# A mixture-of-experts layer: three of five token tiles take their experts from a streamed table instead of gathered rows

## The chip, the cores and the metric

The kernel runs on one core of one Trainium2 chip. The metric is the device time of one execution in microseconds, the median of several. The engines are TensorE (PE; PEld is its weight load), VectorE (DVE), ScalarE (ACT), GpSimd (POOL) and SyncE (SP), which issues DMAs.

## The reference, cut to what matters

One layer of a hybrid backbone for 128 context tokens (tile 0) and 512 latent tokens (tiles 1 to 4), D = 1024, everything in fp32: a gated linear recurrence and an attention, mixed and projected, then PEER, an expert layer with 16384 experts. Only PEER is touched:

```python
def per_block(xb):                                        # 128 tokens
    q = (xb @ w_q).reshape(n, P_HEADS, 2, P_QDIM // 2)    # 8 heads, two halves
    s = jnp.einsum('nhpd,hpkd->nhpk', q, sub_keys)        # 128 keys a half
    s1, i1 = lax.top_k(s[:, :, 0], 16); s2, i2 = lax.top_k(s[:, :, 1], 16)
    ...                                                   # best 16 of the 16 x 16 sums
    idx = jnp.take_along_axis(cand_i, pos, axis=-1)       # expert = i1 * 128 + i2
    g = jax.nn.softmax(top_s, axis=-1)
    u = jnp.take(w_u, idx, axis=0)
    act = jax.nn.gelu(jnp.einsum('nhkd,nd->nhk', u, xb), approximate=False)
    v = jnp.take(w_v, idx, axis=0)
    return jnp.einsum('nhk,nhkd->nd', (g * act), v)
```

Each token so takes 8 x 16 = 128 experts, and the result is the sum over them of gate times gelu(u . x) times v. Around it stand x + gate2 * PEER(...) and a final RMSNorm.

## The kernel before, in words

A slot is one rank of one head for the 128 tokens of a tile: 128 slots a tile, 640 in all. For a slot GpSimd gathers one row of `uv` (u and v side by side, 8 KB) for each token with an indirect DMA (L1213, L1235), 1 MB. VectorE makes the dot of u with the token (L1412), ScalarE its gelu and the product with the gate (L957, L963). The v part is added either by VectorE (L1440) or by TensorE: ScalarE puts the weights on a diagonal (L973), and two products of 128x512 with the gathered rows add up in PSUM (L587, L600).

Before a slot stands the routing of its head on VectorE, in 12 parts (L1347 to L1390): the best 16 of each half, their sums, the best 16 of those, the experts' numbers and the softmax, whose exponential ScalarE makes (L952). It needs the scores, which TensorE makes in `post`.

The program runs through these stages, each engine with its own copy of the order:
- modulation rows, tile 0's projections, mixers, output products and expert scores (`post(0)`);
- projections and mixers of tiles 1 to 4, with the 128 slots of tile 0 beside them. `plan_groups` writes the list of TensorE's groups and a place in it for each slot (`SLOT_AT`, from the shares in `STAGES`), and `Beside` calls the slots at these places on every engine;
- `post(1)` for tile 1 and `post(2)` for tiles 2 to 4: output products (`y`, L859), the normed tile turned (`x2T`, L869), queries (`qp`, L877) and scores (`ss`, L888), with the first 64 slots of tile 1 beside them;
- loops over the other 448 slots (L808 to L833, and their like on PE, ACT and POOL), 32 slots a pass, with eight gather buffers, and for each tile the end: gate, sum with x, RMSNorm, store (`tile_end`, L1685).

Weights come in slabs of 1 MB through a ring of three (`RING`), in the order of `SLABS`. SyncE issues a slab when the last group that reads the ring's place is done (L544).

Of the kernel before, what the change touches and what calls it, by code (L numbers as in the profile page):

```python
# [35 lines left out]
P = 128  # L36
# [18 lines left out]
NGA, NGC, NGB = 4, 6, 8  # L55
HSTATIC = 4
NPE = HSTATIC * TOPK // 2
HSLOTS = 2 * TOPK
# [11 lines left out]
BATCHES = [(0,), (1,), (2, 3, 4)]  # L70
MIXES = [(0,), (1, 2, 3, 4)]
NSLOT = TSLOT + HSTATIC * TOPK
# [6 lines left out]
FIRST_ODD = 9  # L79
# [9 lines left out]
POOL_LEAD, PE_LAG = 3, 2  # L89
# [3 lines left out]
for _b in range(len(BATCHES)):  # L93
    if _b < len(MIXES):
        for _q in range(4):
            SLABS += [("gate_a", _b, _q), ("gate_b", _b, _q), ("wo", _b, _q)]
    SLABS += [("wout", _b, _q) for _q in range(4)] + [("wpq", _b, _q) for _q in range(8)]
    if _b == 0:
        SLABS += [("winTL", w, m) for w in WIN_T for m in range(2)] + [("winL", w, a) for w, a in WIN]

# [19 lines left out]
def turn_order(tiles):  # L120

    order = []
    for i in range(len(tiles) + 1):
        order.extend([("x2T", tiles[i])] if i < len(tiles) else [])
        order.extend([("h2", tiles[i - 1])] if i else [])
    return order


def plan_groups():
# [73 lines left out]
    for b in (1, 2):  # L203
        marks.append(len(names))
        post(b)
    marks.append(len(names))
    marks.insert(-2, names.index(("ss", 1, FIRST_ODD)))
    place, used, fulls, n, six = {}, [0] * 6, [0] * 6, 0, 0
    for name in names:
        kind = name[0]  # L210
        wide = kind in ("xT", "kT", "dS", "qkT", "x2T", "h2") or (kind in ("sc", "pT") and name[1] >= HB)
        if kind in ("oA", "oB"):
            banks = (4 if kind == "oA" else 5,)
        elif six_banks(name):
            banks = (six % 6,)
            six += 1
        else:
# [21 lines left out]
    for (_, count, share), lo, hi in zip(STAGES, marks, marks[1:]):  # L239
        reach = np.cumsum([share[names[i][0]] for i in range(lo, hi)])  # L240
# [14 lines left out]
def build(nc, x_prompt, x_sample, cols, rows, normf_rows, brow, consts, masks, sel, cond_rows, ada_slabs, col_slabs, in_slabs, o_slabs,  # L255
          out_slabs, pq_slabs, uv, state, ckT, cv, y_prompt, y_sample, new_state, new_k, new_v):
    with ExitStack() as ctx:
# [17 lines left out]
        R1 = sb("R1", [P, 4 * D])  # L275
# [5 lines left out]
        RG = sb("RG", [P, 3 * 2 * D])  # L281
        BP = sb("BP", [P, NT * 256 + 6 * 512])
        AB = sb("AB", [P, 12288])
        HG = sb("HG", [P, 5632])
# [4 lines left out]
        CT = sb("CT", [P, P + 640 + NCAND])  # L289
# [6 lines left out]
        hst = sb("hst", [P, 16])  # L296
        ast = sb("ast", [P, 168])
        ZB = sb("ZB", [P, P], BF16)
# [6 lines left out]
        ident, mbias, iota = CT[:, 0:P], CT[:, P:P + 640], CT[:, P + 640:P + 640 + NCAND]  # L305
# [61 lines left out]
        SQ2 = [view(HG, 4096, D), view(HG, D, D), view(HG, D, D)]  # L367
        QP = [view(HG, 5120, 2, P), view(HG, 4096, 2, P), view(HG, 4096, 2, NB[2])]
        X1 = [XP] + [AB[:, 6144 + i * D:6144 + (i + 1) * D] for i in range(4)]
        H2 = [PB[:, 0:D]] + [AB[:, at:at + D] for at in (0, 3072, 4096, 5120)]  # L370
        SC = [R1[:, 0:2048], HG[:, 2048:4096], R1[:, 0:2048], AB[:, 10240:12288], AB[:, 1024:3072]]

        def h_of(b, k):

            return hTp[:, k, :] if b == 0 else hTl[:, k, (BATCHES[b][0] - 1) * P:BATCHES[b][-1] * P]

# [54 lines left out]
        kv_out, state_out, y_out, nf_in, zb_ready = (sem("kv_out"), sem("state_out"), sem("y_out"), sem("nf_in"),  # L431
                                                     sem("zb_ready"))
# [81 lines left out]

        slab_turn, counts = {}, [0] * NSLAB
# [8 lines left out]
        def _(sp):  # L524
            def last_use(key):
# [11 lines left out]

            sp.dma_start(CO[:], cols).then_inc(small_in, 16)
# [1378 lines left out]
```

## Time and profile before

| what | value |
|---|---|
| median of 3 runs | 2538.35 us (2537.91 to 2542.24) |
| profiled execution | span 2543.3 us; the page gives no other time of it |
| TensorE busy | 2005.6 us, 79% |
| TensorE weight load | 1104.9 us, 43% |
| VectorE busy | 1749.4 us, 69% |
| ScalarE busy | 945.2 us, 37% |
| GpSimd busy | 941.2 us, 37% |
| read from HBM | 800.79 MB |
| packets of the gathers' queue | 66.5% of 16 engines' span |
| mean granted clock | 0.924 |

The shares are means over stages with different limits, so the rows below take stretches. A busy TensorE is not TensorE at its peak, since its instructions overlap; the distance between the starts of like groups that follow without a gap is the true cost, and it is read from the rows in order of time. An fp32 product stands in the trace as two records. A record's mean in a group of lines is longer than that distance.

### The profile page before, as it was taken

The numbers are of one execution on the slowest core, as the hardware profiler recorded it, in microseconds if no ns is written. First come the engines' busy times: TensorE is split into PE (matmuls) and PEld (weight loads), VectorE is DVE, ScalarE is ACT, GpSimd is POOL, SyncE is SP. The second block draws the span as 40 slices with busy tenths as digits, with TensorE's granted clock in tenths as the row PEclk, the third lists the DMA queues.
The fourth block names the chain that finished last, engine by engine and source line by source line (L and its number), as shares of the span: only waits on it lengthen the run. The fifth ranks groups of instructions, "written<-read, shape, count | busy, mean of one in ns | idle before, by whom it ended". The sixth has DMA issues, their size and how long they took to land. (4 is left out here: it accounts for less than half of the span.)

```text
span 2543.3 us, 27323 instructions
## 1 busy us (share of the span) xinstructions
PE 2005.6 (79%) x6925; PEld 1104.9 (43%) x6925; DVE 1749.4 (69%) x3969; ACT 945.2 (37%) x2456; POOL 941.2 (37%) x774
## 2 busy tenths in 40 slices
PE   6978898946677798668698776877768787687876
PEld 2577846745566543267455222322223222232222
DVE  2732278886776678767787777777777777777764
ACT  1402145223343434312333444444444444344443
POOL 0020012232222222303233554656545665456654
PEclk9998999977888899879899998999999999999999
DMA  8744678851111389859798999999999999999997
GB/s 317 289 152 154 231 291 322 332 192 67 67 67 60 150 332 337 337 203 401 272 372 317 422 421 393 420 422 422 421 404 415 422 422 421 407 401 421 422 422 330
DMA packets 113299, 805.53 MB, mean 317 GB/s; under 512 B 12596, under 2 KB 14006, under 8 KB 17046
## 3 DMA queue, kind: packets, MB, share of 16 engines
q0 software_dynamic: 93760, 680.96, 66.5%
q1 hardware_dynamic: 17704, 118.17, 12.6%
q10 hardware_dynamic: 1712, 4.98, 0.5%
q8 instruction: 50, 0.82, 0.1%
q14 instruction: 73, 0.60, 0.1%
HBM read 800.79 MB, written 3.28 MB: 316 GB/s over the span
## 5 line engine op out<-in xcount | busy, mean ns | idle before, releaser
L1213 POOL DMA_INDIRECT RG<-in_uv,idxs x264 | 356.5, 1351 | 562.0 <-DVE pl L1440 322.1
L957 ACT ACTIVATE agel<-apre 128x1 f32<-128x1 f32 x640 | 129.3, 202 | 984.6 <-DVE apre L1412 981.2
L600 PE MATMUL pl<-RG,BP 128*128 128x512 f32 x576 | 294.9, 638 | 106.8 <-ACT BP L973 102.3
L600 PE MATMUL pl<-RING,BP 128*128 128x512 f32 x576 | 281.7, 621 | 62.1 <-ACT BP L973 59.6
L1412 DVE CUSTOM_DVE_ANT_0 R<-RG,AB 128x1024 f32<-128x1024 f32 x201 | 246.8, 1230 | 100.8 <-DMA RG<-in_uv,idxs 79.8
L1213 POOL DMA_INDIRECT RING<-in_uv,idxs x168 | 248.9, 1482 | 158.7 <-PE pl L600 69.4
L1412 DVE CUSTOM_DVE_ANT_0 R<-RING,AB 128x1024 f32<-128x1024 f32 x168 | 205.9, 1226 | 95.6 <-DMA RING<-in_uv,idxs 77.2
L625 PE MATMUL pa<-HL,RING 128*128 128x512 f32 (+2 forms) x800 | 243.7, 461 | 4.2 <-DVEq L457 2.6
L600 PEld LDWEIGHTS pl<-RG,BP 128*128 128x128 f32 x576 | 100.1, 192 | 294.5 <-ACT BP L973 214.0
L973 ACT ACTIVATE BP<-CT,wexp 128x128 f32<-128x128 f32 x480 | 192.7, 401 | 51.1 <-PE pl L600 12.9
L600 PEld LDWEIGHTS pl<-RING,BP 128*128 128x128 f32 x576 | 104.3, 194 | 234.2 <-ACT BP L973 139.7
L963 ACT ACTIVATE wexp<-agel,gws 128x1 f32<-128x1 f32 x640 | 188.7, 295 | 22.4 <-ACT agel L957 0.3
L625 PEld LDWEIGHTS pa<-HL,RING 128*128 128x128 f32 x800 | 134.5, 195 | 106.0 <-issue 74.3
L1213 POOL DMA_INDIRECT EB<-in_uv,idxs x88 | 118.3, 1345 | 147.0 <-DVE pl L1440 96.8
L1440 DVE SCALAR_TENSOR_TENSOR pl<-RG,wexp,pl 128x1024 f32<-128x1024 f32 x118 | 151.6, 1285 | 9.6 <-ACT wexp L963 9.5
L1412 DVE CUSTOM_DVE_ANT_0 R<-RG,BP 128x1024 f32<-128x1024 f32 x96 | 117.7, 1226 | 43.4 <-DMA RG<-in_uv,idxs 27.6
L1412 DVE CUSTOM_DVE_ANT_0 R<-EB,AB 128x1024 f32<-128x1024 f32 x67 | 82.4, 1229 | 60.1 <-DMA EB<-in_uv,idxs 58.0
L625 PE MATMUL pa<-RING,AB 128*128 128x256 f32 (+2 forms) x432 | 103.9, 390 | 14.8 <-DVEq L457 10.3
L600 PE MATMUL pl<-HL,BP 128*128 128x512 f32 x192 | 94.9, 617 | 24.9 <-ACT BP L973 22.2
L957 ACT ACT_TABLE_LOAD x86 | 110.3, 1283 | 9.9 <-ACT RING L1096 2.8
L600 PE MATMUL pl<-EB,BP 128*128 128x512 f32 x192 | 98.8, 639 | 11.1 <-ACT BP L973 11.1
L625 PEld LDWEIGHTS pa<-RING,AB 128*128 128x128 f32 (+1 forms) x432 | 82.9, 201 | 34.1 <-issue 17.3
(288 smaller groups left out, 3261.0 us busy)
## 6 DMA issues: line engine op xcount, KB each, us to landing
RING<-in_in_slabs SPq DMA_DIRECT2D x42, 1024.0 KB, 6.0
RING<-in_pq_slabs SPq DMA_DIRECT2D x24, 1152.0 KB, 5.5
RING<-in_ada_slabs SPq DMA_DIRECT2D x16, 1024.0 KB, 5.0
RING<-in_out_slabs SPq DMA_DIRECT2D x12, 1024.0 KB, 9.1
RG<-in_col_slabs POOLq DMA_DIRECT2D x8, 1024.0 KB, 6.9
RING<-in_o_slabs SPq DMA_DIRECT2D x8, 1024.0 KB
RG<-in_uv,idxs POOLq DMA_INDIRECT x297
RING<-in_uv,idxs POOLq DMA_INDIRECT x168
```

Of the source, the lines that this page charges most:

```text
L600: last = nc.tensor.matmul(acc[:, c * 512:(c + 1) * 512], DG[:, k % 2, :], bufs[k % len(bufs)][:, D + c * 512:D + (c + 1) * 512], start=Fal ...
L625: return nc.tensor.matmul(out, l, r, start=s, stop=e)
L957: A(agel[:, par, k:k + 1], apre[:, par, k:k + 1], ACT.Gelu).then_inc(gel_done, 1)
L963: A(wexp[:, par, k:k + 1], agel[:, par, k:k + 1], ACT.Copy, scale=gws[:, par, k:k + 1]).then_inc(w_done, 1)
L973: A(DG[:, i % 2, :], ident, ACT.Copy, scale=wexp[:, par, k:k + 1]).then_inc(dg_done, 1)
L1213: nc.gpsimd.indirect_dma_start(out=bufs[b], out_offset=None, in_=uv, in_offset=bass.IndirectOffsetOnAxis(ap=idxs[:, par, k:k + 1], axis=0) ...
L1412: V.tensor_tensor_reduce(out=SCR[k % 2], in0=buf[:, 0:D], in1=hc, scale=1.0, scalar=0.0, op0=ALU.mult, op1=ALU.add, accum_out=apre[:, par, ...
L1440: V.scalar_tensor_tensor(PL[:, :], (GC[i % NGC] if t else GA[n % NGA])[:, D:2 * D], wexp[:, n // TOPK % 2, n % TOPK:n % TOPK + 1], PL[:, : ...
```

## The change

Tile 0 is computed as before, and tile 1 too, except that all its v sums are made by VectorE, in SBUF, with three gather buffers. Tiles 2 to 4 (`DENSE`, 384 tokens) gather nothing. Expert number i1 * 128 + i2 belongs to chunk c = i2, so there are 128 chunks of 128 experts.
- `U` group of a chunk: eight products of 128x384 give u . x for all 128 experts and 384 tokens; ScalarE's gelu puts it into `AR`, a ring of 42 chunks.
- Gate matrix: for each token TensorE multiplies two one-hot matrices over its 128 chosen experts, 128x128 each, the first one-hot in i1 (GpSimd, `slot_hots`), the second in i2 and weighed by the gate (ScalarE for tiles 2 and 3: Square of the distance, then Relu; VectorE for tile 4). Each product (`G` group, four tokens) is evicted by ScalarE and written to a DRAM buffer, `gates`.
- VectorE multiplies the gelus of 16 chunks with the gates, read back in pieces of 1 MB (`weigh`).
- `V` group of a chunk: six products of 128x512 add up the result of three tiles over all 128 chunks in six PSUM banks.

The three `post` stages become two; tiles 1 to 4 go together. Scores are copied out by ScalarE. x1 of the three tiles goes to DRAM and back. The slots of tile 1 lie beside the V groups, one a chunk.

```diff
-BATCHES = [(0,), (1,), (2, 3, 4)]
+BATCHES = [(0,), (1, 2, 3, 4)]
...
-          ("post1", 0, {"y": 3.5, "x2T": 2.0, "h2": 2.0, "qp": 2.0, "ss": 1.0}),
-          ("queries1", 4, {"qp": 2.0, "ss": 0.1}),
-          ("post2", 60, {"y": 3.4, "x2T": 2.5, "h2": 2.5, "qp": 5.2, "ss": 1.2}))
+          ("post", 0, {}),
+          ("dense", 128, {"V": 1.0, "U": 0.0}))
...
+SLABS += [("dU", p) for p in range(NRING // 2)]
+for _p in range(NCH // 2):
+    SLABS += [("dV", _p)] + ([("dU", _p + NRING // 2)] if _p + NRING // 2 < NCH // 2 else [])
...
+            def gate_slab(b, i):
+                n = b * ND + i
+                if n == 0:
+                    wait_full(sp, ("G", ND - 1, P // 4 - 1))
...
+                if n >= 2:
+                    sp.wait_ge(p_done, n - 1)
+                sp.dma_start(GS[n % 2], gates[b, i]).then_inc(gate_in[n % 2], 16)
...
+            def experts_u(c):
+                w = slab("dU", c // 2)[:, c % 2 * D:(c % 2 + 1) * D]
+                ps = start(("U", c))
+                for k in range(KD):
+                    last = mm(ps[:, 0:DTOK], w[:, k * P:(k + 1) * P], hTl[:, k, P:LAT], k == 0, k == KD - 1)
+                finish(("U", c), last)
+
+            def experts_v(c):
...
+                for i in range(ND):
+                    for x in range(2):
+                        last = nc.tensor.matmul(VACC[i][:, x * 512:(x + 1) * 512], AR[:, c % NRING, i * P:(i + 1) * P],
+                                                w[:, x * 512:(x + 1) * 512], start=c == 0, stop=c == NCH - 1,
+                                                skip_group_check=True)
...
+            def gate_group(i, g):
...
+                for x in range(4):
+                    at = g % 2 * 4 + x
+                    last = mm(ps[:, x * P:(x + 1) * P], OH1[q % 2][:, at, :], OH2[q % 2][:, at, :])
...
             mix(1)
...
             post(1)
-            post(2)
-            beside.rest()
...
+            for c in range(12):
+                experts_u(c)
+            for i in range(ND):
+                turn_slots(i)
+                for g in range(0, P // 4, 4):
+                    for x in range(4):
+                        gate_group(i, g + x)
+                    if i < ND - 1:
+                        experts_u(12 + i * 8 + g // 4)
+            for c in range(NEARLY, NRING):
+                experts_u(c)
...
+            for c in range(0, NCH, 2):
+                experts_v(c)
+                experts_v(c + 1)
+                for n in (c + NRING, c + NRING + 1):
+                    if n < NCH:
+                        experts_u(n)
...
+            def gate_hots(i, q):
...
+                for x in range(ONEHOT):
+                    at = q * ONEHOT + x
+                    step.post(A(to[:, x, :], iota_p, ACT.Square, bias=by[:, 1, at:at + 1]))
+                step.settle()
+                for x in range(ONEHOT):
+                    at = q * ONEHOT + x
+                    step.post(A(to[:, x, :], to[:, x, :], ACT.Relu, bias=by[:, 2, at:at + 1], scale=by[:, 3, at:at + 1]))
+                step.settle(oh2a_ready)
...
+                gate_hots(i, 0)
+                for h in range(PH):
+                    for q in (2 * h, 2 * h + 1):
+                        if q + 1 < P // ONEHOT:
+                            gate_hots(i, q + 1)
+                        gates_out(i, 2 * q)
+                        gates_out(i, 2 * q + 1)
+                    gelu_u(12 + i * PH + h)
+                    expos(turn_of(DENSE[i + 1], h))
...
+            def weigh(b, i):
+                n = b * ND + i
+                dve.wait_ge(act_ready, GBLK * (b + 1))
+                dve.wait_ge(gate_in[n % 2], 16 * (n // 2 + 1))
...
+                    step(V.tensor_tensor(to, to, gate[:, lo:lo + m, :], ALU.mult))
...
+            for i, t in enumerate(DENSE):
+                for h in range(PH):
+                    dve.wait_ge(sc_ready, 2 * PH + 2 * h + 2)
...
+                    route(t, h, 0, 12)
+                slots_of(i)
+            for q in range(P // ONEHOT):
+                gate_hots(ND - 1, q)
```

TensorE's order after the scores of `post(2)`, in the kernel before: the last slots beside the queries (L587) and the first of the loops (L600). `HL` holds the turned tiles, `BP` the diagonal, `RG`, `EB`, `RING` and `HL` the gathered rows, `po` and `pl` the sums in PSUM.

```order
L625 MATMUL pa<-HL,RING 128x384 x8
L587 MATMUL po<-RG,BP 128x512 x2
L625 MATMUL pa<-RING,HG 128x128 x6
L587 MATMUL po<-EB,BP 128x512 x2
L600 MATMUL po<-RING,BP 128x512 x6
L600 MATMUL po<-HL,BP 128x512 x2
```

TensorE's order in the changed kernel, one pair of chunks in the middle of the dense pass and the start of the next: `AB` is the ring of weighed gelus, L972 the V groups, L689 the U groups.

```order
L972 MATMUL po<-RING,AB 128x512 x2
L972 MATMUL pl<-RING,AB 128x512 x2
L972 MATMUL pa<-RING,AB 128x512 x2
L972 MATMUL po<-RING,AB 128x512 x2
L972 MATMUL pl<-RING,AB 128x512 x2
L972 MATMUL pa<-RING,AB 128x512 x2
L689 MATMUL pa<-HL,RING 128x384 x16
L972 MATMUL po<-RING,AB 128x512 x2
```

Two products a slot have become six and eight products a chunk, with nothing of another kind between them.

ScalarE's order in the last slots of the kernel before: gelu, gate, diagonal.

```order
L957 ACTIVATE agel<-apre 128x1
L963 ACTIVATE wexp<-agel,gws 128x1
L973 ACTIVATE BP<-CT,wexp 128x128
L957 ACTIVATE agel<-apre 128x1
L963 ACTIVATE wexp<-agel,gws 128x1
```

ScalarE's order in the changed kernel, one block of 16 tokens of tile 2: `XS` is a buffer of one-hots, `G` the turned slot lists, L1299 the evictions of the gate products, L1259 the gelu of a U group, L1049 the exponential of a head of tile 3.

```order
L1285 ACTIVATE XS<-CT,G 128x128 x8
L1289 ACTIVATE XS<-XS,G 128x128 x8
L1299 ACTIVATE AB<-pa 128x8x64 x2
L1285 ACTIVATE XS<-CT,G 128x128 x8
L1289 ACTIVATE XS<-XS,G 128x128 x8
L1299 ACTIVATE AB<-pa 128x8x64 x2
L1302 DMA gates<-AB 128x8x256
L1259 ACT_TABLE_LOAD
L1259 ACTIVATE AB<-pa 128x384
L1049 ACT_TABLE_LOAD
L1049 ACTIVATE BP<-BP 128x16
```

The one-hots, the evictions, a gelu and the exponential on which VectorE's routing waits stand in one queue.

## Rows read from the trace of the kernel before

**Rows 1.** Busy time by stage (instructions), clock, DMA share, GB/s
```profile
1094.60:1260.00 165.40, 129.84 (x657) 105.82 (x656) 117.47 (x277) 44.49 (x115) 31.25 (x30) 0.87 0.75 290
1260.00:1387.00 127.00, 126.73 (x430) 74.04 (x428) 107.03 (x246) 41.94 (x125) 37.65 (x35) 1.00 0.91 351
1387.00:2531.80 1144.80, 892.49 (x1841) 324.33 (x1841) 818.61 (x1982) 495.78 (x1469) 654.28 (x448) 0.97 1.00 413
```

**Rows 2.** TensorE in order of time: start, length, line, shape, records [idle before]
```profile
1093.78 1.01 PE L894 MATMUL po<-ZB 128*128 128x128 bf16 x8 [27.41 <-DVEq L457]
1094.58 16.55 PE L625 MATMUL pa<-RING,AB 128*128 128x256 f32 x64
...
2502.00 1.98 PE L600 MATMUL pl<-HL,BP 128*128 128x512 f32 x4 [0.50 <-ACT BP L973]
```

**Rows 3.** TensorE in order of time, gapless groups
```profile
229.24 7.31 PE L625 MATMUL pa<-EB,RING 128*128 128x128 f32 x64
...
236.39 3.74 PE L625 MATMUL pa<-HG,RING 128*128 128x128 f32 x32
...
917.96 27.63 PE L625 MATMUL pa<-HL,RING 128*128 128x512 f32 x64
...
945.43 7.03 PE L625 MATMUL po<-AB,RING 128*128 128x512 f32 x16
...
1260.44 5.32 PE L625 MATMUL pa<-HL,RING 128*128 128x384 f32 x16
1265.60 1.88 PE L587 MATMUL po<-RG,BP 128*128 128x512 f32 x4
```

**Rows 4.** TensorE and VectorE in order of time, tile 1's turning
```profile
1121.05 4.94 PE L625 MATMUL pa<-HL,RING 128*128 128x128 f32 x32
...
1117.13 1.75 DVE L1732 TENSOR_SCALAR HL<-pa,AM,ADA 128x128 f32<-128x128 f32 x4 [2.12 <-PE pa L628]
```

**Rows 5.** VectorE in order of time, tile 0's first head
```profile
323.14 0.29 DVE L1350 COPY BP<-R 128x256 f32<-128x256 f32 x1
...
336.47 0.29 DVE L1350 COPY BP<-R 128x256 f32<-128x256 f32 x1
```

**Rows 6.** ScalarE by line and shape: count, busy us, mean ns, idle before
```profile
L973 ACT ACTIVATE BP<-CT,wexp 128x128 f32<-128x128 f32 x480 | 192.7, 401 | 51.1 <-PE pl L600 12.9 <-ACT wexp L963 1.2 <-PE po L600 1.0
...
L1013 ACT ACTIVATE HL<-pa,ADA,AM 128x128 f32<-128x128 f32 x32 | 14.6, 457 | 5.2 <-PE pa L628 4.3
...
L1115 ACT ACTIVATE HG<-pa 128x512 f32<-128x512 f32 x10 | 6.0, 597 | 0.1
...
L1150 ACT ACTIVATE HG<-pa 128x384 f32<-128x384 f32 x16 | 7.8, 489 | 39.4 <-PE pa L625 39.4
...
L952 ACT ACT_TABLE_LOAD x40 | 51.3, 1283 | 1.0 <-ACT HG L1150 0.3
...
L952 ACT ACTIVATE BP<-BP 128x16 f32<-128x16 f32 x40 | 12.3, 307 | 10.7 <-DVEq L1369 10.2
...
L952 ACT ACTIVATION_READ_ACCUMULATOR BP<-BP 128x1 f32 x40 | 7.5, 186 | 0.0
...
L1057 ACT ACTIVATE HG<-pa 128x1024 f32<-128x1024 f32 x5 | 5.1, 1023 | 37.1 <-PE pa L628 36.8 <-ACT RING L1096 0.3
```

**Rows 7.** GpSimd and VectorE by line and shape
```profile
L1255 POOL TENSOR_TENSOR HG<-HG 128x128 f32<-128x128 f32 x5 | 2.3, 468 | 0.4
...
L1552 DVE TENSOR_SCALAR BP<-BP,LB 128x128 f32<-128x128 f32 x8 | 2.8, 346 | 7.6 <-ACTq L457 7.4
```

**Rows 8.** Busy time in two stretches of 100 us, as rows 1
```profile
300.00:400.00 100.00, 99.33 (x370) 55.48 (x369) 63.86 (x161) 38.70 (x69) 18.08 (x18) 1.00 0.82 301
...
500.00:600.00 100.00, 56.03 (x291) 48.24 (x289) 82.30 (x165) 31.09 (x77) 28.74 (x35) 0.78 0.47 168
```

**Rows 9.** VectorE in order of time, end of the last tile
```profile
2534.30 1.23 DVE L1698 TENSOR_TENSOR R<-pl,G 128x1024 f32<-128x1024 f32 x1 [3.59 <-PE pl L894]
```

**Rows 10.** DMA issues: queue, count, KB, median us to landing
```profile
RING<-in_out_slabs SPq DMA_DIRECT2D x12, 1024.0 KB, 9.1
```

More of the change, by code:

```diff
@@ L124, in turn_order @@
         order.extend([("x2T", tiles[i])] if i < len(tiles) else [])
-        order.extend([("h2", tiles[i - 1])] if i else [])
+        order.extend([("h2", tiles[i - 1])] if i and tiles[i - 1] < 2 else [])
     return order
@@ L216, in plan_groups @@
             six += 1
+        elif at > first_v:
+            banks = (late % 2,)
+            late += 1
         else:
@@ L1150, in post, with gelu_u @@
                     step(A(QP[b][:, m % 2, :], ps[:, 0:N], ACT.Copy), *freed(("qp", b, m)), qp_ready)
-                    if b == 1 and m == 6:
-                        expos(PH)
+                    if m:
+                        scores_out(m - 1)
+                scores_out(2 * PH - 1)
+            def gelu_u(c):
+                ps = group(("U", c))
+                if c == 0:
+                    act.wait_ge(x1_out, 16 * ND)
+                if c == NEARLY:
+                    for s in stage_out:
+                        act.wait_ge(s, 16 * (ND * P // GTOK // 2))
+                step(A(AR[:, c % NRING, :], ps[:, 0:DTOK], ACT.Gelu), *freed(("U", c)), act_ready)
@@ new lines, in gates_out @@
+            def gates_out(i, g):
+                ps = group(("G", i, g))
+                s, turn = block_of(i, g)
+                if g % 4 == 0 and turn:
+                    act.wait_ge(stage_out[s], 16 * turn)
+                to = STG[s].rearrange("p b (t c) -> p b t c", c=GBLK)[:, :, g % 4 * 4:g % 4 * 4 + 4, :]
+                step(A(to, ps.rearrange("p (t b c) -> p b t c", t=4, c=GBLK), ACT.Copy), *freed(("G", i, g)))
+                if g % 4 == 3:
+                    at = g // 4 * GTOK * GBLK
+                    act.dma_start(gates[:, i, :, at:at + GTOK * GBLK].rearrange("b p n -> p b n"),
+                                  STG[s]).then_inc(stage_out[s], 16)
@@ new lines, in sums, with route @@
+            def sums(groups):
+                for c, i0, rows_, w in groups:
+                    r(V.tensor_tensor(RCC[:, :, c:c + rows_ * w].rearrange("p t (a b) -> p t a b", a=rows_),
+                                      RVI[:, :, i0:i0 + rows_].unsqueeze(3).to_broadcast([P, 2, rows_, w]),
+                                      RVI[:, :, TOPK:TOPK + w].unsqueeze(2).to_broadcast([P, 2, rows_, w]),
+                                      ALU.add))
+            def route(t, h, lo, hi):
+                j, turn = t * PH + h, turn_of(t, h)
+                for i in range(lo, hi):
@@ L1806, in _ @@
+            step(V.memset(ACC, 0.0))
+            route(1, 0, 0, 11)
+            for b in range(2):
+                for i in range(ND):
+                    weigh(b, i)
+            route(1, 0, 11, 12)
+            route(1, 1, 0, EARLY)
+            beside.open(1)
+            for b in range(2, NBLK):
+                beside.before(("V", GBLK * b - 12))
+                weigh(b, 0)
+                weigh(b, 1)
+                beside.before(("V", GBLK * b - 8))
+                weigh(b, 2)
             beside.rest()
-            dve.wait_ge(h2_ready, NT)
```

617 lines of the change are left out of this document (311 added, 306 removed).

## The prediction, made before the changed kernel ran

> **What bounds the kernel now.** I read the busy shares first, then the slices. The whole-span shares (PE 79%, DVE 69%) name no bound, because the program has stages with different limits. The busy times by stage do [rows 1]. From 1094.6 us on there are three. Up to 1260 and up to 1387 us TensorE works on tile 1's and then tiles 2 to 4's output products and expert queries, in the second of these at full clock and 127 of 127 us busy. From 1387 to 2531.8 us the DMA share is 1.00 at 413 GB/s: 448 slots (640 less tile 0's 128 and the first 64 of tile 1) fetch 1 MB each, so one takes 1144.8/448 = 2.56 us. TensorE's own record there is four half-products per slot at 1.98 us with half a microsecond of wait between [rows 2]: it is covered, but not by much. The reader is to see that TensorE has little time to give in either stage.
>
> **The change part by part.** Up to 1094.6 us (the first output product of tile 1 [rows 2]) both kernels run the same order; the score copies go to ScalarE and each head loses a 0.29 us copy, worth -5 to +5 us, taken as 0, since tile 0's slots there pace themselves by their gathers. What goes: 384 of the slots of tiles 2 to 4, and the third pass over the query weights. What stays: 128 slots of tile 1, now beside the dense pass. What comes is mostly TensorE work, so its prices come first, from starts that follow each other without a gap [rows 3]:
> - eight products of 128x384: 1265.60 - 1260.44 = 5.16 us (16 records);
> - eight of 128x512: (945.43 - 917.96)/4 = 6.87 us, so six take 5.15;
> - one of 128x128: (236.39 - 229.24)/32 = 0.223 us;
> - eight of 128x256, the half of 6.87: 3.44 us.
>
> The 64 records of 128x512 in the 917.96 row are 32 products, two records each, so a column costs 1.7 ns, and the dense pass has no narrower type: the tables stay fp32.
>
> A floor first, with every wait at nothing. The dense pass has 128 chunks, each with a U group (8 x 384) and a V group (6 x 512): 128 x (5.16 + 5.15) = 1320 us. The gate matrices add 384 products of 128x128, 86 us. Outputs are 16 x 3.44 = 55, queries and scores 16 x (6.87 + 4 x 0.223) = 124, the end 22 (below). 1094.6 + 1320 + 86 + 55 + 124 + 22 = 2702 us, already 159 us over the span of before: the kernel trades 384 x 2.56 = 983 us of DMA for 1406 us of an engine that was not free to take it.
>
> Now the stages in the order of the program, with their waits.
>
> Stage A, outputs of four tiles: 55 us, plus 3 for the lower clock after the 27 us gap [rows 2] (four groups took 16.55 there, 13.8 at full clock). To 1153.
>
> Stage B, norm and turn of four tiles. One tile took 10 us, from the end of its output products (1094.58 + 16.55 = 1111.1) to 1121.05 [rows 2, 4]; each further one adds VectorE's half of the turned tile (1.75), its scaling and their waits, some 3 us: 19. To 1172. Bounds 13 (all hidden) to 27.
>
> Stage C, queries and scores: 124 us plus 3 for the last copies. ScalarE makes two 0.6 us copies in each 7.76 us, VectorE waits. To 1299. VectorE gets ready-made scores here, but head 0 of tile 2 stops at the exponential, which ScalarE issues only behind all of stage C.
>
> Stage D, routing of tile 2. A head took 336.47 - 323.14 = 13.33 us [rows 5]; without the score copy and the cast to integer it is 12.6. Seven heads behind stage C: 88 us and 2 for the tokens' slot lists: to 1389. TensorE covers 12 U groups, 62 us, and then waits 28.
>
> Stage E, gate matrices of tiles 2 and 3, 16 blocks of 16 tokens. ScalarE leads. Per token it makes a Square and a Relu over 128x128. The nearest rows are 0.401 us with one pointer and 0.457 with two [rows 6], 0.86 together, but those wait for one another, and the new ones go out eight in a row. A 1024-column copy takes 1.023 and a 512-column one 0.597, so 128 columns alone are 0.107, 0.21 for both: the lower end. I take 0.70, nearer to the rows. Per block: 16 x 0.70 = 11.2, four 128x512 evictions 2.4, one gelu of 128x384 0.5, one exponential with two table loads 2 x 1.28 + 0.31 + 0.19 = 3.1; 17.2 us. Beside it lie VectorE's head (12.6), GpSimd's 16 one-hot rows (0.47 each at most by its 128x128 row [rows 7], 7.5) and TensorE's four groups and one U group (3.6 + 5.2). TensorE works half of such a block; a stretch with PE busy 56% was granted 0.78 [rows 8], and at 1.2 GHz the U group ends behind ScalarE's second set, which then waits up to 6 us. I add 3 for this and the handshakes: 20 us a block, 320 for 16, 6 to start, 3 between tiles. To 1718. Bounds: 15 us a block (columns alone, then VectorE's head and its exponential set the pace) to 26 (0.86 per token, and all U groups at 1.2 GHz).
>
> The Trainium skill (ScalarE: Activation LUTs, What ACT_TABLE_LOAD costs) says that a pointer operand costs 93 ns and that back-to-back ACTIVATEs overlap by 93 ns; by its figures a token costs some 0.68 us, which would take 5 us from the sum. It also puts a switch of table sets at 2.66 us with its drain; the rows show 1.28 and the next activation right behind. By the page stage E would be 44 us longer.
>
> Stage F, tile 4. VectorE makes the second one-hot, 0.35 us each by its 128x128 row with two pointers [rows 7]; GpSimd the first. 16 groups of 8 at 3 us, plus start: 50 us, bounds 35 to 75. To 1768.
>
> Stage G, U groups 28 to 41: 14 x 5.16 = 72. To 1840. Under it run the first six weighings (TENSOR_TENSOR of 128x2048, 2.45 us each by the 1.23 us row of 1024 [rows 9]) and the first gate loads. A late one would cost a few us.
>
> Stage H, 128 V groups and 86 U groups in pairs: 214 x 5.16 = 1104 us, clock 1.00, as in the stretch with 99% busy [rows 8]. To 2944. What lies beside it, per pair of chunks (20.6 us): two 1 MB slabs, two slots, 0.4 MB of gates: 4.4 MB, 11 us at 413 GB/s. VectorE: two slots of 2.5 us, 1.6 of routing, 0.9 of weighing, 7.5 us. What is queued behind the new waits: ScalarE runs a slot of tile 1 ahead of the gelu of a U group, so a late gather holds the gelu, that holds the bank of the next U group but one, with 10 us to spare. SyncE waits for a weighing before a gate load, and slabs stand behind it; VectorE is a pair ahead there. Upper bound for the stage +60 us, lower 0.
>
> Stage I: the end. One tile's end took 2543.3 - 2534.3 = 9 us, the store included [rows 9]. Three follow each other at 6 us each, then the store and 1 us to start: 22. Span 2966 us. The page gives the profiled execution by its span alone, 5 us over the median of the runs (2538.35), so the time is 2961, say 2960 us. A difference of 0.2% is 5 us, about what a measurement can tell.
>
> **The rivals.**
> Slow gate building: 26 us a block. For it: the clock that falls in half-busy stretches [rows 8] and the rows of 0.40 and 0.46 us. Against: eight activations in a row don't wait for each other. 16 x 6 more: 3056 us.
>
> Fast gate building: 15 us a block, VectorE sets the pace. 16 x 5 less: 2880 us.
>
> Stalls in the dense pass: slabs share the queues with 128 gathers. For it: output slabs landed in 9.1 us at the median [rows 10]. Against: three slabs in the ring give a load two pairs' half, 20 us. A loss of 1 us a pair is 64 us: 3025 us.
>
> The other side, not slower: a dense group takes far less than 5.16 us, because products that stream with resting weights and one operand in the ring run at one pass a column. Its place is stage H. Every group of 5.16 us would be 2.6; 214 x 2.58 = 552 us, which gives about 2410 us. It decides from a group of (2543.3 - 22 - 1840)/214 = 3.2 us down. Against it stands every gapless row: two records of 0.32 us for 384 columns. The Trainium skill (TensorE: Matmul & The Clock Gate, Back-to-back issue gap) gives N/2.4 + 2.5 ns for a matmul, 162 ns at 384 columns, which is this rival's price if a product is one such matmul. The trace has two records a product at twice that each, so it does not hold for fp32 here.
>
> **How the numbers follow.** Forecast as summed, 2900 to 3015 by itself: 0.70. Slow building 0.12, fast building 0.10, stalls 0.06, the other side 0.02. The range from 2870 to 3060 us takes in the two ways of building and the stalls. Faster by over 0.2%: 0.02; within 0.2%: 0.01; slower: 0.97, since the floor alone is slower.
>
> **What would show it.** In the profile after: TensorE at 98% or more and clock 1.00 over the last 1100 us, with V and U groups of 5.15 us; DMA share there near 0.55; ScalarE over 80% busy for some 320 us before, TensorE near 45%; a gap of TensorE near 28 us behind U group 11; VectorE heads of 12.6 us behind stage C and of 20 us beside stage E. I am wrong if the dense stage is not gapless, if blocks of 16 tokens take under 15 or over 26 us, or if a dense group does not cost 5.16 us.

## The result: 3003.8 us, 18% slower than before

The changed kernel takes 3003.83 us (median of four runs, 2999.84 to 3010.76), the kernel before 2538.13 beside it. The ratio is 1.184, 95% interval 1.182 to 1.187, so 466 us are lost. The forecast was 2960, with a range from 2870 to 3060: 44 us short, and in the range.

Lines of the changed kernel's profile page come first: busy shares, the span in 40 slices, and what was read from HBM.

```profile
span 3003.4 us, 28511 instructions
...
PE 2520.2 (84%) x9022; PEld 1542.2 (51%) x9022; DVE 1510.6 (50%) x3327; ACT 854.0 (28%) x1952; POOL 663.4 (22%) x773
...
PE   7969988567779858994656569999999999999996
...
ACT  2321342334343321135989521101010010101100
...
PEclk9979999788889978996777769999999999999998
...
HBM read 543.92 MB, written 30.02 MB: 191 GB/s over the span
```

TensorE is at nine tenths or more from the 25th slice to the 39th. ScalarE has its nine, eight and nine in slices 20 to 22. The busy times by stage answer to [rows 1]; the stages are those of the prediction, A to H and then the end. H's last product ends at 2975.3; its window runs to 2980 here, and takes in most of tile 1's end.

```profile
1090.60:1149.00 58.40, 57.24 (x256) 49.79 (x256) 26.83 (x53) 1.98 (x4) 0.58 (x1) 0.97 0.23 79
1149.00:1167.40 18.40, 8.04 (x41) 6.63 (x41) 11.55 (x27) 8.56 (x18) 0.00 (x0) 0.68 0.29 116
1167.40:1294.40 127.00, 127.00 (x384) 64.00 (x385) 9.41 (x36) 18.52 (x31) 0.00 (x0) 0.98 0.19 68
1294.40:1388.00 93.60, 64.71 (x194) 37.24 (x192) 70.06 (x273) 30.22 (x45) 0.00 (x0) 0.87 0.22 79
1388.00:1700.60 312.60, 183.30 (x774) 141.59 (x774) 161.20 (x618) 273.36 (x663) 194.71 (x256) 0.76 0.24 81
1700.60:1799.20 98.60, 54.76 (x259) 50.48 (x260) 46.25 (x158) 19.19 (x33) 90.38 (x128) 0.61 0.22 75
1799.20:1872.20 73.00, 73.00 (x227) 42.98 (x226) 26.11 (x15) 8.26 (x15) 2.93 (x3) 0.99 0.59 230
1872.20:2980.00 1107.80, 1103.11 (x2913) 553.08 (x2911) 448.40 (x693) 127.06 (x377) 152.19 (x125) 1.00 0.65 237
2980.00:3003.40 23.40, 0.00 (x0) 0.00 (x0) 17.03 (x22) 0.61 (x3) 0.00 (x0) 0.50 0.26 105
```

Three stages carry the result. H, the last but one, is TensorE's alone: 1103 of 1108 us busy at full clock, DMA share 0.65 where [rows 1] had 1.00. E (1388 to 1700.6) is ScalarE's, 273 of 313 us. F (1700.6 to 1799.2) is GpSimd's, 90 of 99 us.

The dense pass in TensorE's order, against the gapless rows of [rows 3]:

```profile
1872.19 1.88 PE L972 MATMUL po<-RING,AB 128*128 128x512 f32 x4
...
1882.49 10.48 PE L689 MATMUL pa<-HL,RING 128*128 128x384 f32 x32
1892.81 1.88 PE L972 MATMUL po<-RING,AB 128*128 128x512 f32 x4
```

Two V groups take 10.30 us, two U groups 10.32: 5.15 and 5.16 each, to the digit what the kernel before paid.

ScalarE in stage E, one block of 16 tokens, against [rows 6]:

```profile
1451.77 2.43 ACT L1285 ACTIVATE XS<-CT,G 128x128 f32<-128x128 f32 x8
1454.23 3.19 ACT L1289 ACTIVATE XS<-XS,G 128x128 f32<-128x128 f32 x8
1457.60 1.31 ACT L1299 ACTIVATE AB<-pa 128x512 f32<-128x512 f32 x2 [0.18 <-ACT XS L1289]
...
1466.62 1.28 ACT L1259 ACT_TABLE_LOAD   x1 [0.50 <-ACT AB L1299]
1467.92 0.49 ACT L1259 ACTIVATE AB<-pa 128x384 f32<-128x384 f32 x1
1468.58 1.28 ACT L1049 ACT_TABLE_LOAD   x1 [0.17 <-ACT AB L1259]
1469.88 0.31 ACT L1049 ACTIVATE BP<-BP 128x16 f32<-128x16 f32 x1
1470.09 0.19 ACT L1049 ACTIVATION_READ_ACCUMULATOR BP<-BP 128x1 f32 x1
1470.19 0.97 ACT L1285 ACTIVATE XS<-CT,G 128x128 f32<-128x128 f32 x3
```

From 1451.77 to 1470.19 is 18.42 us a block, and ScalarE is busy in 17.4 of it.

GpSimd in stage F makes the eight first one-hots of a group, and TensorE waits for them:

```profile
1725.77 5.64 POOL L1392 TENSOR_SCALAR EB<-CT,G 128x128 f32<-128x128 f32 x8 [0.20 <-POOL EB L1392]
1731.61 5.64 POOL L1392 TENSOR_SCALAR EB<-CT,G 128x128 f32<-128x128 f32 x8 [0.20 <-POOL EB L1392]
```
```profile
1731.51 2.97 PE L689 MATMUL pa<-XS,EB 128*128 128x128 f32 x16 [2.21 <-POOLq L516]
1737.35 3.78 PE L689 MATMUL pa<-XS,EB 128*128 128x128 f32 x16 [2.86 <-POOLq L516]
```

That is 5.84 us a group; one comparison, with the multiplication in the same instruction, costs GpSimd 5.64/8 = 0.70 us.

### The profile page after: what moved, and what is told of

It reads as the page before. It is cut to its first block, busy times and chain, and to the rows that moved or that the text cites. A ratio compares the mean times of both kernels' runs of the same rounds, so it can differ in the third digit from the quotient of the medians.

```text
span 3003.4 us, 28511 instructions
## 1 busy us (share of the span) xinstructions
PE 2520.2 (84%) x9022; PEld 1542.2 (51%) x9022; DVE 1510.6 (50%) x3327; ACT 854.0 (28%) x1952; POOL 663.4 (22%) x773
## 4 chain that ended last, share of the span: by engine, by line
PE 55%; DVE 16%; DMA 12%; issue 9%; POOL 7%; ACT 1%; DVEq 0%; SPq 0%; POOLq 0%; ACTq 0%
PE pa L689 37%; DMA R<-in_uv,idxs 9%; POOL EB L1392 6%; PE pa L972 5%; PE pl L972 5%; PE po L972 5%; DVE pl L1594 3%; PE po L689 1%; PE pa L692 1%; DVE AB L1723 1%; DVE AB L1731 1%; DVE AB L1594 1%; DMA RING<-in_ada_slabs 1%; DMA EB<-in_uv,idxs 1%; DVE BP L1508 1%
## 5 line engine op out<-in xcount | busy, mean ns | idle before, releaser
L689 PE MATMUL pa<-HL,RING 128*128 128x384 f32 (+1 forms) x2592 | 923.8, 515 | 12.3 <-ACTq L516 7.9
L689 PEld LDWEIGHTS pa<-HL,RING 128*128 128x128 f32 x2592 | 498.3, 194 | 420.5 <-issue 166.5
L1377 POOL DMA_INDIRECT R<-in_uv,idxs x224 | 265.4, 1185 | 1353.6 <-DVE AB L1594 996.6
L1594 DVE SCALAR_TENSOR_TENSOR AB<-R,wexp,AB 128x1024 f32<-128x1024 f32 x128 | 164.2, 1282 | 432.4 <-ACT wexp L1061 432.2
L1392 POOL TENSOR_SCALAR EB<-CT,G 128x128 f32<-128x128 f32 x384 | 285.1, 761 | 409.0 <-ACTq L516 334.8
L1259 ACT ACTIVATE AB<-pa 128x384 f32<-128x384 f32 x128 | 62.9, 491 | 837.0 <-PE pa L689 836.1
L689 PE MATMUL pa<-XS,EB 128*128 128x128 f32 x768 | 148.4, 372 | 164.4 <-POOLq L516 90.9
L1571 DVE CUSTOM_DVE_ANT_0 R<-R,G1L 128x1024 f32<-128x1024 f32 x128 | 156.8, 1225 | 208.3 <-DMA R<-in_uv,idxs 156.9
L972 PE MATMUL pl<-RING,AB 128*128 128x512 f32 x512 | 240.6, 592 | 0.0
L972 PE MATMUL pa<-RING,AB 128*128 128x512 f32 x512 | 240.6, 592 | 0.0
L972 PE MATMUL po<-RING,AB 128*128 128x512 f32 x512 | 240.6, 592 | 0.0
L689 PEld LDWEIGHTS pa<-XS,EB 128*128 128x128 f32 x768 | 139.5, 279 | 175.9 <-POOLq L516 97.1
L689 PE MATMUL pa<-RING,AB 128*128 128x256 f32 (+3 forms) x656 | 137.2, 357 | 44.7 <-DVEq L516 40.9
L972 PEld LDWEIGHTS pa<-RING,AB 128*128 128x128 f32 x512 | 97.3, 190 | 122.5 <-issue 122.5
L972 PEld LDWEIGHTS pl<-RING,AB 128*128 128x128 f32 x512 | 97.3, 190 | 122.4 <-issue 122.4
L689 PE MATMUL pa<-AB 128*128 128x128 f32 (+2 forms) x736 | 119.4, 324 | 44.9 <-DVEq L516 28.1
L972 PEld LDWEIGHTS po<-RING,AB 128*128 128x128 f32 x512 | 97.3, 190 | 113.1 <-issue 101.4
L689 PEld LDWEIGHTS pa<-RING,AB 128*128 128x128 f32 (+1 forms) x656 | 114.7, 195 | 70.1 <-DVEq L516 31.4
L689 PEld LDWEIGHTS pa<-AB 128*128 128x128 f32 (+2 forms) x736 | 106.5, 227 | 59.3 <-issue 27.3
```

Source lines behind the costliest of these rows:

```text
L689: return nc.tensor.matmul(out, l, r, start=s, stop=e)
L972: last = nc.tensor.matmul(VACC[i][:, x * 512:(x + 1) * 512], AR[:, c % NRING, i * P:(i + 1) * P], w[:, x * 512:(x + 1) * 512], start=c == ...
L1259: step(A(AR[:, c % NRING, :], ps[:, 0:DTOK], ACT.Gelu), *freed(("U", c)), act_ready)
L1377: nc.gpsimd.indirect_dma_start(out=bufs[b], out_offset=None, in_=uv, in_offset=bass.IndirectOffsetOnAxis(ap=idxs[:, par, k:k + 1], axis=0) ...
L1392: step.post(nc.gpsimd.tensor_scalar(OH1[n % 2][:, x, :], iota_p, SLT[:, i % 2, 0, at:at + 1], 1.0, ALU.is_equal, ALU.mult))
L1571: V.tensor_tensor_reduce(out=SCR[k % 2], in0=bufs[b][:, 0:D], in1=hc, scale=1.0, scalar=0.0, op0=ALU.mult, op1=ALU.add, accum_out=apre[:, ...
```

## The experiments

Each is the changed kernel with one edit, unless said otherwise. Where a ratio stands, it is to the kernel before on the same chip; the changed kernel's own is 1.184. The kernel before took 2532 to 2539 us in the different sets of runs, so stages are compared by their lengths. "V starts" is TensorE's first V group, 1872.2 in the changed kernel. Runs 1, 2 and 4 to 6 were timed once each, the others four times or more.

**1. Half of the V groups' columns.** What one dense group is worth.

```
-for x in range(2):      # V groups: two halves of 512 columns
+for x in range(1):
```

> Leaves out the second 512 columns of every V group (three products of 128x512 a chunk instead of six); the rest stays. Theory: TensorE's column count sets the dense stage (1872.2 to 2975.1 us in the changed kernel). 128 V groups at 2.58 us instead of 5.15 are 330 us less: 3003 to 2673 us. The last 42 V groups then take 108 us, and tile 1's last 42 slots, each 3.5 to 5 us, can't hide behind them, so up to 60 us come back: 2673 to 2735. Rival, the stage is set by slabs, gathers and their waits: less than 100 us go, over 2900.

Measured: 2780.1 us, 224 less, short of the 330 that 128 groups of half the length give, and 45 above the upper end expected. The trace says where the rest went:

```profile
1872.00:2500.00 628.00, 628.00 (x1789) 340.04 (x1788) 297.64 (x482) 92.59 (x270) 99.04 (x82) 1.00 0.78 295
2530.00:2755.00 225.00, 109.70 (x251) 47.77 (x249) 128.31 (x177) 25.25 (x90) 43.60 (x39) 0.75 0.79 293
```

While U groups still come, TensorE is without a gap, 628 of 628 us: the price of a group is as said, and a DMA share of 0.78 takes nothing from it. When only V groups are left, tile 1's slots fall behind: the last 40 start from 2536.4 to 2746.2, 5.4 us apart. TensorE is through at 2677, having been idle for 38 us of stage H, and 77 us of slots follow it. VectorE waits there for gathers:

```profile
2710.83 1.22 DVE L1571 CUSTOM_DVE_ANT_0 R<-R,G1L 128x1024 f32<-128x1024 f32 x1 [2.60 <-DMA R<-in_uv,idxs]
...
2714.45 1.23 DVE L1571 CUSTOM_DVE_ANT_0 R<-R,G1L 128x1024 f32<-128x1024 f32 x1 [1.19 <-DMA R<-in_uv,idxs]
...
2719.53 1.23 DVE L1571 CUSTOM_DVE_ANT_0 R<-R,G1L 128x1024 f32<-128x1024 f32 x1 [2.65 <-DMA R<-in_uv,idxs]
```

Two slots take 8.7 us here. In the changed kernel the last 40 slots start 5.3 us apart beside V groups of 5.15, so they are close to being the bound there too, which bears on its end (run 7).

**2. No Relu in tiles 2 and 3.** The second operation on each one-hot left out.

```
-for x in range(ONEHOT): step.post(A(to[:, x, :], to[:, x, :], ACT.Relu, bias=..., scale=...))
-step.settle(oh2a_ready)
+act.sem_inc(oh2a_ready, 1)
```

> Leaves out the Relu of the weighed one-hots of tiles 2 and 3 on ScalarE (the Square stays): 16 of the 32 one-hot activations a block. Theory: ScalarE sets the 16 blocks of the gate building (18.4 us each, 3.19 us of Relu twice). They fall to 13 to 14.5 us, where VectorE's head of 12.6 us and the wait for its exponential take over: 62 to 86 us less, 2917 to 2941. Rival, GpSimd sets them: it takes 5.8 us for eight one-hots and stood idle 6 us a half-block only because TensorE was late; then a block stays above 17 us and the gain is under 25 us.

Measured: 2932.6 us, and the block falls from 18.4 to 13.7 us. ScalarE sets stage E. V starts at 1796.5, 76 us earlier: 10 of them lie before stage E, and 65 are its own (247.4 us instead of 312.6). The time is 71 us less. I had expected VectorE's head to set the block then. The trace has GpSimd fill it: its two sets of eight take 5.6 and 6.5 us, each behind 0.8 us of wait for TensorE, while ScalarE waits 1.8 us for a U group.

**3. Upper halves.** All four operands of the dense groups are read as bf16, the upper two bytes of each fp32; loads unchanged. The dense products have bf16 operands then, where the reference and both kernels have fp32.

```
+def upper(a): return a.bitcast(BF16).rearrange("p (n two) -> p n two", two=2)[:, :, 1]
-mm(ps[:, 0:DTOK], w[...], hTl[...], ...)      # and the V product alike
+mm(ps[:, 0:DTOK], upper(w[...]), upper(hTl[...]), ...)
```

> The U and V groups read only the upper halves of their fp32 operands, as bf16 with a stride of two (the lower 16 bits are left out of these products; same bytes moved, same columns). Theory: an fp32 column costs four cycles, a bf16 column one, so a group falls from 5.16 to about 1.3 us, and the dense stage from 1103 to what stands next: 107 slabs, 128 gathers and 20 gate pieces of 1 MB, 268 MB, 650 us at 413 GB/s; stage G from 73 to 25 to 45. Whole: 2500 to 2590 us. Rival, bf16 at a stride of two streams at half rate: a group 2.6 us, H about 650 as well, whole under 2620, told apart by the records. Rival, something else than the columns set the stage: over 2800 us.

Measured: 2621.3 us, ratio 1.033 (1.031 to 1.034), 31 us above the upper end expected. Its TensorE rows stand first: 16 records for two U groups, one a product, and 2.70 us for the two where fp32 takes 10.32. Then come the whole stage, and VectorE's group in it:

```profile
2002.34 2.86 PE L689 MATMUL pa<-HL,RING 128*128 128x384 bf16 x16 [1.80 <-ACTq L516]
2005.04 0.61 PE L975 MATMUL po<-RING,AB 128*128 128x512 bf16 x2
2005.49 0.61 PE L975 MATMUL pl<-RING,AB 128*128 128x512 bf16 x2
```
```profile
1833.00:2592.00 759.00, 373.89 (x1456) 157.62 (x1456) 441.73 (x687) 125.33 (x374) 136.21 (x125) 0.75 0.88 344
```
```profile
L1574 DVE CUSTOM_DVE_ANT_0 R<-R,G1L 128x1024 f32<-128x1024 f32 x128 | 156.9, 1226 | 301.5 <-DMA R<-in_uv,idxs 253.7 <-issue 40.0 <-DVE BP L1469 2.9
```

TensorE works half of the 759 us. It is through at 2507, and the last 18 slots take the 85 us behind it, so slots end the stage now: 759/128 = 5.9 us each. VectorE waits 254 us for gathers that share the queues with slabs, and TensorE's U groups wait 224 us for ScalarE, in whose queue their gelus stand behind the slots'. Without slabs, from 2507 on, a slot takes 4.6 us, at a DMA share of 0.64. How much of the 5.9 us is the queues' and how much the three gather buffers', no run separates.

**4 to 6. What GpSimd's comparison costs.** Three edits of its one instruction.

```
 nc.gpsimd.tensor_scalar(OH1[...], iota_p, SLT[:, i % 2, 0, at:at + 1], 1.0, ALU.is_equal, ALU.mult)
4: a constant 5.0 for the pointer SLT[...] (no one-hot comes out)
5: ALU.mult, ALU.add for ALU.is_equal, ALU.mult (nor here)
6: None, ALU.is_equal: the comparison alone
```

> GpSimd's first one-hot compares with a constant instead of the token's column of numbers (the gates are then wrong; the same count, shape and operations). It measures what the pointer operand costs: 761 ns mean now. Theory A, the pointer makes the row dear: the mean falls to 0.3 to 0.5 us, tile 4's building from 98.6 to 55 to 70 us, the whole 30 to 40 us less, 2963 to 2973. Theory B, comparison and multiplication over 128 columns cost this on GpSimd with any operand: the mean stays over 0.65 us and the time within 8 us of 3003.

Measured: 3004.4 us, and in stage F a group of eight starts every 6.0 us. The pointer costs nothing.

> GpSimd's one-hot operation multiplies by its pointer and adds a constant where it compared and multiplied; same shape, same pointer, no one-hot comes out, so the gates are left out of what is computed. Theory A (the comparison is what makes the row 0.70 to 0.76 us): by the 512-column row of the same two arithmetic operations (0.618 us) 128 columns take 0.2 to 0.4 us, VectorE's eight second one-hots of some 0.31 us set tile 4's pace, 2.6 to 3.4 us a group, and the time is 3004 - 16 x 2.9 = 2950 to 2970 us. Theory B (a pointer row of 128 columns costs it 0.7 us whatever it computes): 3000 to 3006 us.

Measured: 2950.3 us, 53.5 less; 7 us of this come before stage F, which takes 52.4 us instead of 98.6. Its rows:

```profile
1735.26 2.80 POOL L1392 TENSOR_SCALAR EB<-CT,G 128x128 f32<-128x128 f32 x8 [0.20 <-POOL EB L1392]
1738.27 2.80 POOL L1392 TENSOR_SCALAR EB<-CT,G 128x128 f32<-128x128 f32 x8 [0.20 <-POOL EB L1392]
```

Same shape, same pointer, two operations: 0.35 us instead of 0.70. A group takes 3.0 us, what the prediction took. I had expected VectorE to set this pace. Its own eight take 2.85 us here and GpSimd's 2.80, and neither engine waits over 0.2 us between them, so which of the two holds the other at 3.0 us is not shown.

> GpSimd compares only, without the multiplication by one behind it. Theory A (two operations in one pass, each an instruction's work to this engine, make the price): the row falls from 0.70 to 0.4 to 0.5 us, the group of eight in tile 4 from 5.84 to 3.5 to 4 us, the time to 2966 to 2975 us. Theory B (the comparison alone is the price): no change, 3000 to 3006 us.

Measured: 2980.6 us, 23 less, of which 7 come before stage F. A group takes 4.9 us, and stage F 83.4:

```profile
1729.66 4.74 POOL L1392 TENSOR_SCALAR EB<-CT,G 128x128 f32<-128x128 f32 x8 [0.20 <-POOL EB L1392]
1734.60 4.66 POOL L1392 TENSOR_SCALAR EB<-CT,G 128x128 f32<-128x128 f32 x8 [0.20 <-POOL EB L1392]
```

Neither theory holds as written: the row falls to 0.59 us only. The comparison is the dear part, the multiplication behind it 0.1 us of the 0.70.

**7. Slots spread evenly.** Tile 1's 128 slots are counted against U and V groups alike.

```
-("dense", 128, {"V": 1.0, "U": 0.0})
+("dense", 128, {"V": 1.0, "U": 1.0})
```

> Tile 1's 128 slots are spread over U and V groups alike by TensorE's time and not by V groups alone. Theory A (tile 1's last 42 slots run at 5.2 us each against 42 V groups of 5.155 and so end with the stage, which puts tile 1's end behind it): tile 1's end leaves the tail, 6.6 us less, 2995 to 2999 us. Theory B (the tail is 28 us because four ends follow each other whatever the slots do, or a slot costs TensorE something wherever it stands): 3002 to 3006 us.

Measured: 2994.8 us, ratio 1.181 (1.178 to 1.184), so the two intervals overlap a little. The trace is clearer than the time:

```profile
2970.69 1.22 DVE L1851 TENSOR_TENSOR R<-po,G 128x1024 f32<-128x1024 f32 x1 [82.56 <-PE pa L972]
```

VectorE has been idle for 83 us and then ends tile 2 as soon as TensorE's last product is there. From 2970.7 to the span's end are 21.5 us, where the changed kernel has 28.1. The other 4.7 us by which this execution is shorter lie before its first V group (1867.5), where the edit changes nothing. In the changed kernel tile 1's last slot comes with the last V groups, and its end goes first:

```profile
2971.44 1.23 DVE L1571 CUSTOM_DVE_ANT_0 R<-R,G1L 128x1024 f32<-128x1024 f32 x1 [2.92 <-DMA R<-in_uv,idxs]
...
2975.33 1.22 DVE L1851 TENSOR_TENSOR R<-AB,G 128x1024 f32<-128x1024 f32 x1
...
2981.95 1.22 DVE L1851 TENSOR_TENSOR R<-po,G 128x1024 f32<-128x1024 f32 x1 [0.76 <-DMA R<-x1s]
```

2981.95 - 2975.33 = 6.6 us of a fourth end in the tail.

**8. Exponentials of tile 2 between the score copies.** In stage C instead of behind it.

```
 for m in range(2 * PH):                         # the copies of stage C
+    if b and m >= 4 and m % 2 == 0: expos(turn_of(DENSE[0], m // 2 - 2))
...
-for h in range(PH): expos(turn_of(DENSE[0], h)); (one or two of gelu_u)
+for c in range(12): gelu_u(c)
```

> The exponentials of tile 2's heads are issued on ScalarE between the score copies of the queries stage, not behind all of them. Theory A (the 28 us of TensorE's wait in the routing of tile 2 come from heads that start only when ScalarE is through with the score copies): VectorE's heads begin during the queries stage, the first gate block begins some 28 us earlier, and everything behind it moves with it: 3004 - 28 = 2976 us, 2970 to 2982. Theory B (VectorE's own work on the heads, 12.6 us each, sets the routing whatever ScalarE does, because VectorE is held by tile 1's slots in the queries stage): 2998 to 3006 us.

Measured: 2974.0 us, ratio 1.172 (1.170 to 1.175). TensorE turns tile 2's lists right behind its twelfth U group and no longer after two gaps; the row of the changed kernel stands second:

```profile
1292.70 62.09 PE L689 MATMUL pa<-HL,RING 128*128 128x384 f32 x192
1354.62 0.49 PE L692 MATMUL pa<-CT,BP 128*128 128x128 f32 x3
```
```profile
1388.05 0.90 PE L692 MATMUL pa<-CT,BP 128*128 128x128 f32 x3 [21.03 <-DVEq L1534]
```

It is 33 us earlier, and V starts 33 us earlier too; 2 of them lie before stage A.

**9. One-hots of tile 4 shared.** GpSimd makes three of each eight, VectorE five besides its own eight.

```
-for x in range(ONEHOT):                              # GpSimd
+for x in range(FPOOL if i == ND - 1 else ONEHOT):    # FPOOL = 3; the others on VectorE
```

> In tile 4 GpSimd makes three of each eight first one-hots and VectorE the other five beside its eight second ones. Theory A (GpSimd's comparison at 0.70 to 0.76 us a row is the whole of what tile 4's gate building took over the forecast): GpSimd 3 x 0.73 = 2.2 us a group of eight, VectorE 13 x 0.32 = 4.2 us, so 16 groups fall from 5.84 to 4.2 to 4.5 us and the stage from 98.6 to 68 to 77 us: 2972 to 2982 us. Theory B (the hand-over between the engines and TensorE at the lower clock sets the 5.84 us): no change, 3000 to 3006 us.

Measured: 2960.8 us, ratio 1.167 (1.164 to 1.169), 11 us better than the lower end expected. A group takes 3.43 us and stage F 58.1. VectorE makes 13 rows in 3.43 us, 0.26 us each, where I had 0.32; GpSimd's three take 0.83 each beside it:

```profile
1731.94 2.49 POOL L1393 TENSOR_SCALAR EB<-CT,G 128x128 f32<-128x128 f32 x3 [0.95 <-PE pa L690]
```

**10. Runs 7, 8 and 9 in one**, all in fp32.

> The early exponentials, the shared one-hots of tile 4 and the evenly spread slots together, everything in fp32. Theory A (the three savings lie in stages that follow each other and each is on the path that sets the end): they add. Measured one by one against the changed kernel's 3004: -30, -43 and -9, so 2922 us, 2915 to 2930, still some 385 us slower than before, since 1320 us of dense products remain. Theory B (a stage that follows hides part of one, as when slots bind behind a faster TensorE): 2935 to 2960 us.

Measured: 2922.1 us (2914.0 to 2924.5), ratio 1.150 (1.147 to 1.153). They add. Some 384 us over the kernel before remain, with the 1320 us of dense products untouched.

**11. Upper halves with all three.**

> The dense groups read the upper halves of their fp32 operands as bf16, with the early exponentials, the shared one-hots and the evenly spread slots. By the sum of the parts measured so far: 2621 (upper halves alone) - 28 - 26 = 2567, and the dense stage may give or take some with the other spread of slots: 2530 to 2575 us, near or above the 2537 of before. If the dense stage is set by 128 slots of 5.9 us wherever they stand, that sum holds at 2567. If it was set by slots that stood beside V groups alone, and slabs and slots now share the stage evenly, it falls by up to 757 - 128 x 5.2 = 90 us: about 2480 us, faster than before.

Measured: 2524.1 us, ratio 0.995 (0.993 to 0.997), nine runs against fourteen. With bf16 operands in the dense products this beats both kernels, the one before by 11 us. It is 43 us under the sum written ahead of it. Of these, 17 are run 9's, which gave 43 us and not the 26 of that sum. For the other 26 the even spread is a candidate, tested next.

**12. The same without the even spread.**

> The upper-half kernel with early exponentials and shared one-hots, but with tile 1's slots counted against V groups alone, as in the changed kernel. It tells where the last run's 43 us below the sum of its parts came from. Theory A (the slots spread evenly start in the U groups ahead of the first V group and so the slots, which bind this stage, begin some 40 us earlier): 2550 to 2575 us. Theory B (the gain is in the early exponentials and one-hots, and 128 slots of 6.0 us bind in either spread): 2515 to 2535 us.

Measured: 2521.9 us, ratio 0.994 (0.991 to 0.996): the same time. The spread gives nothing here. The rows that turn tile 2's lists show what gave the rest: they stand at 1386.73 with upper halves alone, and at 1320.46 with the early exponentials as well.

```profile
1386.73 0.90 PE L692 MATMUL pa<-CT,BP 128*128 128x128 f32 x3 [25.80 <-DVEq L1537]
```
```profile
1320.46 0.49 PE L693 MATMUL pa<-CT,BP 128*128 128x128 f32 x3
```
```profile
1730.00:2495.00 765.00, 376.54 (x1456) 158.41 (x1456) 447.90 (x694) 125.67 (x376) 138.09 (x125) 0.74 0.88 344
```

That is 66 us (4 of them before stage A), where the sum had 28 and the fp32 kernel got 33: there twelve U groups of 5.16 us stood in the way. Stages F and G give 37 more (103.8 us, where run 3 took 141.1), where the sum had 26. From the first V group to the end of the last slot are 759 us here (1730.2 to 2489.2; the row's window takes in tile 1's end), 759 in run 3 and 767 in run 11. TensorE's last product comes 86 us before the last slot's end here, and 28 us with the even spread of run 11: slots end the stage in either, and what it begins earlier arrives at the end.

## Why the prediction was right, and the term that was mis-sized

**The bound.** Right: TensorE's dense products, at prices that the trace of before held. G and H were put at 72 + 1104 us and took 73 + 1103. TensorE over 98% busy, clock 1.00, groups of 5.15 and 5.16 us are all there. DMA share was put near 0.55 and is 0.65, with no loss: the rival of stalls in the dense pass is out, and run 1 shows TensorE gapless at 0.78 too.

**Stages A to D.** 58, 19, 127 and 90 us were forecast; 58.4, 18.4, 127.0 and 93.6 came. Stage A begins 4 us earlier than taken, inside the 5 us allowed for that. TensorE's gap of 28 us in D is two, 7.2 and 21.0. Its cause, that heads wait for exponentials queued behind the copies of stage C, is shown by run 8.

**Stage E.** 20 us a block were taken, 18.4 came, 313 us against 329. ScalarE sets it (run 2). A token costs (2.43 + 3.19)/8 = 0.70 us, as taken; of the 3 us added for waits on U groups at the lower clock 1.2 came (18.4 against 17.2). TensorE was busy 59% there, not near 45%. Both rivals, 15 and 26 us a block, are out. The Trainium skill (ScalarE: Activation LUTs, What ACT_TABLE_LOAD costs) gives, as an estimate by its figures, 0.68 us for a token, and the trace agrees within 4%. Its 2.66 us for a switch of table sets does not hold here: from the end of one activation to the start of the next, load included, are 1.8 us before the gelu and 1.5 before the exponential.

**Stage F, the term that failed.** The step was "GpSimd the first. 16 groups of 8 at 3 us, plus start: 50 us, bounds 35 to 75". It took 98.6, outside its bounds. I had priced GpSimd by its multiplication of two 128x128 tiles [rows 7], 0.468 us "at most", and expected VectorE to set the pace. Runs 4 to 6 show why that row was the wrong neighbour: on this engine the operation decides. A multiplication and an addition over 128x128 take 0.35 us, a comparison alone 0.59, a comparison and a multiplication 0.70. With the cheap operation stage F takes 52.4 us, near the 50 forecast; so 46 of the 49 us are the price of the comparison. In stage E the same row, 0.76 us at the mean, lay under ScalarE's block and cost 1.3 us at most (312.6 us, 311.3 with the cheap operation).

**Stage I.** 22 us were taken for three ends, and 28.1 came, from the last V group's end to the span's. Tile 1's last slot came with the stage's end, so four ends follow each other (run 7: 21.5 us when the slots are done before). I had counted 2.5 us of VectorE a slot; with the wait for its gather it is 5.3 there, and 5.4 in run 1. That three buffers for the gathers are what holds it there is an argument, not shown: no run had more buffers.

**The sum.** F +48.6, I +6.1, D +3.6, E -16.4, the start -4.0, the others within 1 us each: +38, and 2966 + 38 = 3004, against a span of 3003.4. So two errors of opposite sign stand in it, and that the time came out within 44 us of 2960 is in part luck: stage F alone would have put it 49 off. The page's span lies 0.4 us under the median here, where it lay 5 over in the kernel before; that correction, made in the forecast, added 5 to the miss of the time.

**The other side.** The rival was products of one record, at 2.6 us a group. In fp32 none came. With bf16 operands (run 3) a product is one record, and a U group is cheaper still: 1.35 us, 8 records of 0.169. The run also shows why the rival's 2410 us would not have come even then: slots of 5.9 us take over as the bound at 759 us for the stage. The Trainium skill (TensorE: Matmul & The Clock Gate, Back-to-back issue gap) gives 162 ns for 384 columns; the bf16 records are within 4% of it, while each fp32 product is two records at twice that, and it does not hold for them. The prediction called 162 ns this rival's price, which was a slip: eight of them are 1.3 us, half of the rival's group.

## What to carry to other kernels

Before trading gathered bytes for dense products, sum the products at the gapless price of the same type and shape: here that floor alone lay 159 us above the kernel before, and no scheduling got back more than 82. Price an operation by a row with the same operation on the same engine, not only the same shape; where none is there, leave the upper bound open. Once the bound is lifted, ask what the next one costs in place (the gathered slots here), since it decides how much of a large cut arrives.

## What the runs showed of the hardware

- GpSimd's tensor-scalar over 128x128 fp32: 0.35 us for multiply and add, 0.59 for a comparison, 0.70 for a comparison and multiply, the pointer free. The first was measured beside a VectorE without gaps; the last was 0.83 beside one (run 9).
- VectorE's comparison and multiplication over 128x128 took 0.26 us in a row of 13 (run 9) and 0.36 beside GpSimd's multiply and add (run 5). The 0.35 of [rows 7] is a multiplication and an addition.
- With every second bf16 of an fp32 tile read, in both operands, TensorE took 0.225 us for 512 columns at clock 1.00, where an fp32 product takes 0.86. No run reads bf16 without the stride, so whether the stride costs anything is not shown.
- A slot whose rows are gathered took 4.6 to 4.7 us with nothing but slots on the queues, at a DMA share near 0.65 (runs 1, 3 and 12), and 5.9 beside slabs (run 3).
- In fp32 the stage H kept its full clock with slots, gathers and slabs beside it; in bf16, half busy, it was granted 0.75.
